# Hybrid encoder layer, one core: first loads in halves on two queues, memory columns turned inside the chunks

## The reference, cut to what matters

```
mkv = mem @ w_mem_kv[l]            # (256 x 2048) @ (2048 x 2048), float32
mk, mv = jnp.split(mkv, 2, axis=-1)
```

## Time and profile before

| | us |
|---|---|
| median of the runs (lowest, highest) | 1850.0 (1849.56, 1850.88) |
| span of the profiled execution | 1848.4 |
| TensorE busy | 1825.4 (99%) |
| VectorE busy | 1311.8 (71%) |
| ScalarE busy | 864.8 (47%) |
| GpSimd busy | 206.5 (11%) |
| mean granted TensorE clock | 0.996 |

### The profile page before, as it was taken

The page is one execution under the profiler, slowest core; times in us unless marked ns, Lnnn a source line. Parts: engine busy times, 40 slices in busy tenths (PEclk is TensorE's granted clock), DMA queues, the critical chain, the costliest instruction groups (busy, mean ns, idle before and its releaser), DMA issues.

```text
span 1848.4 us, 24154 instructions
## 1 busy us (share of the span) xinstructions
PE 1825.4 (99%) x8577; PEld 1512.7 (82%) x8577; DVE 1311.8 (71%) x2076; ACT 864.8 (47%) x1461; POOL 206.5 (11%) x279
## 2 busy tenths in 40 slices
PE   9999999999999999999999999999999999999995
PEld 7888888888888888888888888888888888888884
DVE  5777765887767675566678878878787644576776
ACT  4653333554555554444445545545455333235543
POOL 1111110000111110000000000000001000003223
PEclk9999999999999999999999999999999999999998
DMA  9576677963643433444273360533619445439988
GB/s 327 186 206 179 185 196 219 224 216 78 176 113 97 119 91 109 117 129 129 65 215 105 147 218 25 213 103 126 227 46 319 150 154 178 145 110 233 243 210 192
DMA packets 227415, 301.49 MB, mean 163 GB/s; under 512 B 13633, under 2 KB 140673, under 8 KB 225153
## 3 DMA queue, kind: packets, MB, share of 16 engines
q1 hardware_dynamic: 171824, 188.24, 32.1%
q0 software_dynamic: 55360, 111.61, 22.7%
q10 hardware_dynamic: 144, 0.52, 0.1%
HBM read 247.73 MB, written 50.97 MB: 162 GB/s over the span
## 4 chain that ended last, share of the span: by engine, by line
PE 95%; DMA 2%; ACT 1%; DVE 1%; POOL 1%; issue 0%; DVEq 0%; SPq 0%; POOLq 0%; ACTq 0%
PE acc L667 10%; PE acc L669 10%; PE acc L668 10%; PE scores L862 6%; PE scores L858 6%; PE scores L860 6%; PE acc L862 3%; PE acc L860 3%; PE acc L858 3%; PE transposed L692 3%; PE scores L1102 2%; PE scores L1103 2%; PE scores L1101 2%; PE attended L860 2%; PE attended L862 2%; PE attended L858 2%
## 5 line engine op out<-in xcount | busy, mean ns | idle before, releaser
L1289 ACT ACTIVATE piece_split<-w 128x512 fp32r<-128x512 f32 x448 | 282.5, 632 | 288.8 <-PE scores L862 105.3
L1849 DVE TENSOR_TENSOR piece_split<-w,piece_split 128x512 fp32r<-128x512 f32 x448 | 308.8, 691 | 110.3 <-ACT piece_split L1289 98.5
L1703 DVE TENSOR_TENSOR w_lo<-raw_weights,w_hi 128x1024 fp32r<-128x1024 f32 x181 | 220.3, 1220 | 179.8 <-ACT w_hi L1184 178.8
L667 PE MATMUL acc<-h_hi,w_lo 128*128 128x512 f32 x800 | 319.4, 399 | 0.0
L669 PE MATMUL acc<-h_hi,w_hi 128*128 128x512 f32 x800 | 312.4, 391 | 0.0
L668 PE MATMUL acc<-h_lo,w_hi 128*128 128x512 f32 x800 | 311.6, 389 | 0.0
L1184 ACT ACTIVATE w_hi<-raw_weights 128x1024 fp32r<-128x1024 f32 x181 | 191.2, 1059 | 191.4 <-PE acc L1103 52.2
L669 PEld LDWEIGHTS acc<-h_hi,w_hi 128*128 128x128 f32 x800 | 150.1, 188 | 32.4
L667 PEld LDWEIGHTS acc<-h_hi,w_lo 128*128 128x128 f32 x800 | 150.8, 189 | 29.9 <-issue 1.8
L668 PEld LDWEIGHTS acc<-h_lo,w_hi 128*128 128x128 f32 x800 | 150.6, 188 | 28.4
L858 PE MATMUL scores<-piece_split,h_lo 128*128 128x512 f32 x384 | 149.6, 390 | 0.0
(11 more groups left out here) (447 smaller groups left out, 3677.7 us busy)
## 6 DMA issues: line engine op xcount, KB each, us to landing
w<-in_w_in SPq DMA_DIRECT2D x128, 512.0 KB, 7.4
raw_weights<-in_w_in SPq DMA_DIRECT2D x102, 512.0 KB, 3.8
raw_weights<-in_w_branch SPq DMA_DIRECT2D x48, 512.0 KB, 5.2
raw_weights<-in_w_mem_kv SPq DMA_DIRECT2D x32, 512.0 KB, 6.1
gate<-gate_scratch POOLq DMA_DIRECT2D x12, 1024.0 KB, 6.7
h_sums<-sums_scratch POOLq DMA_DIRECT2D x6, 1024.0 KB, 10.4
gate_scratch<-first_product POOLq DMA_DIRECT2D x12, 512.0 KB, 6.5
out_w_x<-in_w_out POOLq DMA_DIRECT2D x12, 512.0 KB, 7.8
```

What stands on the lines that cost most here:

```text
L667: pe.matmul(bank_out, wl, hi[:, k, :], start=first, stop=False)
L1289: act.activation(p_split[:, n % RING, 0, :], sources[p][:, k, :], ACT.Copy).then_inc(pc_hi, 1)
L1703: dve.tensor_tensor(w_lo[:, slot, :], raw[:, slot, :], w_hi[:, slot, :].bitcast(F32), ALU.subtract).then_inc(lo_ready, 1)
L1849: dve.tensor_tensor(p_split[:, n % RING, 1, :], sources[p][:, k, :], p_split[:, n % RING, 0, :].bitcast(F32), ALU.subtract).then_inc(pc_lo, 1)
```

## The change

Loads. SyncE now issues memory columns 0 to 255 (256 KB), the second half of chunk 0 (256 KB), memory columns 256 to 511 (256 KB), chunks 1 and 2, memory columns 512 to 1023, chunk 3, columns 1024 to 1535, chunk 4, columns 1536 to 2047, chunk 5 and on. The first half of chunk 0 (256 KB) is issued by ScalarE, ahead of its first copy.

TensorE. Six warming matmuls in place of 8, fill 0, five more, chunk 0. Fill 1 stands between the halves of chunk 0, fills 2 and 3 behind the first and the second half of chunk 1, fill 4 behind chunk 2, fills 5 and 6 behind the halves of chunk 3, fill 7 between the halves of chunk 4. Chunk 1 is split and waited for in halves too.

ScalarE and VectorE. The order becomes memory part 0, chunk 0 in halves, memory part 1, chunk 1 in halves, chunk 2, memory part 2, chunk 3, part 3, chunk 4, part 4, chunk 5, part 5, parts 6 and 7, chunk 6 and on.

Semaphores. `ident_made` and the masks' one are one, as are the two of the last half stores; counts are raised to match.

The diff, cut to its core:

```diff
-            load_mem(0)
-            load_k(0)
+            load_mem(0, 1, mem_loaded[0])
+            sp.dma_start(raw[:, 0, 512:CW], w_mem_kv[0][P:2 * P, 0:512]).then_inc(raw_loaded[0], 16)
+            load_mem(1, 2, mem_second_loaded)
             load_k(1)
-            load_mem(1)
             load_k(2)
+            load_mem(2, 4, mem_loaded[1])
             load_k(3)
-            load_mem(2)
-            load_mem(3)
+            load_mem(4, 6, mem_loaded[2])
             for n in range(4, 8 * HC):
                 load_k(n)
+                if n == 4:
+                    load_mem(6, 8, mem_loaded[3])
...
-            for n in range(8):
+            for n in range(6):
                 pe.matmul(ob[:, 0:P], ident[:, :], ident[:, :], start=True, stop=True)
             fill_mem(0)
-            fill_mem(1)
             for n in range(5):
                 pe.matmul(ob[:, 0:P], ident[:, :], ident[:, :], start=True, stop=True)
-            mem_chunk(0)
-            fill_mem(2)
-            fill_mem(3)
-            mem_chunk(1)
-            fill_mem(4)
-            fill_mem(5)
-            mem_chunk(2)
-            fill_mem(6)
-            fill_mem(7)
-            for n in range(3, 8 * HC):
+            mem_chunk(0, {0: lambda: fill_mem(1)})
+            mem_chunk(1, {0: lambda: fill_mem(2), 1: lambda: fill_mem(3)})
+            mem_chunk(2, {1: lambda: fill_mem(4)})
+            mem_chunk(3, {0: lambda: fill_mem(5), 1: lambda: fill_mem(6)})
+            mem_chunk(4, {0: lambda: fill_mem(7)})
+            for n in range(5, 8 * HC):
...
+            act.dma_start(raw[:, 0, 0:512], w_mem_kv[0][0:P, 0:512]).then_inc(first_loaded, 16)
             mem_part(0)
...
+            for n in range(2):
+                act.wait_ge((first_loaded, raw_loaded[1])[n], 16)
+                act.activation(w_hi[:, n, 0:512], raw[:, n, 0:512], ACT.Copy).then_inc(first_hi, 1)
+                act.wait_ge(raw_loaded[n], 16)
+                act.activation(w_hi[:, n, 512:CW], raw[:, n, 512:CW], ACT.Copy).then_inc(hi_ready, 1)
+                if n == 0:
+                    mem_part(1)
+            for n in range(2, 6):
+                split_hi(n - LOOKAHEAD)
+                mem_part(n)
```

## The result

The changed kernel takes 1852.98 us in the median (1852.18 to 1854.57), the kernel before beside it 1850.65 us: ratio 1.0013, 95% interval 1.0008 to 1.0019. It is 2.3 us slower, clear of noise and under 0.2%. The forecast was 1849.8 with a range to 1852.0. It started from a median of 1850.0 for the kernel before; against its own start it allowed for -0.2 us and at most 2.0, and the runs moved by +2.3. The profiled execution spans 1850.5 us against 1848.4.

What follows compares the result with a forecast made beforehand. TensorE's start was taken to bound the kernel: -1.57 us from an earlier chunk 0, +0.44 for fill 1, +0.9 for a wait at chunk 1, in sum -0.2, giving 1849.8 us. The range was 1847.9 to 1852.0.

Steps and rivals of the forecast that it cites:

- Reading of the bound: Whole kernel: a microsecond by which TensorE's first real matmul starts earlier is a microsecond of the result, unless lost in the stream.
- Term 1: First loads, halved and on two queues: memory columns land at 4.6 us, weights at 5.7 (bounds 5.0 to 6.9).
- Rival B: First loads: weights land late, at 6.9, as the second queue doesn't speed them; +0.7 us, 1850.7; chance 0.2.
- Term 2: Start of TensorE: two warming matmuls fewer end the warming 0.9 us earlier, at 4.4, beside the wait for the load.
- rival C: Start of TensorE: slow pace lasts into chunk 0, six matmuls 1.46 us more, fills and copies 0.3 to 0.4; 1851.6; chance 0.1.
- Term 3: Fill 0 to chunk 0's first matmul: 2.9 us, so chunk 0 starts at 7.5; gain so far 1.57 us.
- Terms 4 and 5: Chunks 0 and 1: fill 1 now inside the stream costs 0.44 us, a new wait ahead of chunk 1 costs 0.9.
- term 6: Memory columns 512 to 1023 and 1536 to 2047 load later: nothing, given 4.7 us of slack; otherwise 1.3 us per load.
- Terms 6 and 7: Memory loads moved back in the queue, and semaphores joined: both put at nothing.
- rival D: Chunks 2 to 8: 1 KB pieces or the reordered queue starve the stream; 4 us of loss, 1854; chance 0.03.

Runs made afterwards that it cites:

- e3: Changed kernel with the first half of chunk 0 issued on SyncE's queue, not ScalarE's: 0.7 us faster than before (ratio 0.9985 to 1.0003).
- e13: Changed kernel with SyncE's second and later loads held until ScalarE's first half of chunk 0 landed: 0.2 us slower than before (0.9993 to 1.0012).
- e6: Changed kernel with 17 warming matmuls in place of 6: 3.0 us slower than before (ratio 1.0005 to 1.0023).
- e4: Changed kernel with memory columns 0 to 511 in one load of 2 KB pieces, still two queues: 3.7 us slower than before (1.0010 to 1.0028).
- e7b: Changed kernel with only 32 KB of chunk 0's first half on ScalarE's queue, the rest on SyncE's: 0.7 us faster than before (0.9986 to 1.0004).
- e2: Kernel before with only the new order of work, its loads kept on one queue: 2.0 us slower than before (ratio 1.0002 to 1.0020).
- e9: Kernel before with GpSimd's six small loads held until chunk 0's rows landed: 0.3 us slower than before (ratio 0.9991 to 1.0009).
- e5: Kernel before with chunk 0's rows loaded in two halves on SyncE's queue: 0.4 us faster than before (ratio 0.9990 to 1.0008).
- e1: Kernel before with only the new loads, its order of work kept: 2.7 us slower than before (ratio 1.0003 to 1.0021).

## Why the prediction was wrong, step by step

- **Reading of the bound: right.** TensorE's start is carried through to 1785 us almost unchanged (2.98, then 3.07). What I left out is that the tail, which is bound by loads, gives nearly 1 us back (3.07 late at its first load, the spans 2.1 apart).
- **Term 1, the half-size loads: the step that failed.** I put the columns' landing at 4.6 and gave bounds only to the weights' landing (5.0 to 6.9). It was 7.2 for the columns and 7.1 for the weights. The working added up bytes, as if a load were announced when they and some more had moved; e3 shows that this is nearly so on one queue (3.6, when I had allowed 4.2), and e13 that with two queues it is so only while nothing else is queued (4.7 and 4.9). With the later loads queued it is not. Rival B was nearest, with later loads served among the first ones, but it was priced for the weights alone. Its bound of 6.9, put on the columns, gives 6.9 + 2.9 = 9.8 for chunk 0; the measured start of fill 0 gives 7.3 + 2.9 = 10.2, and 10.54 was measured. That bytes served in between were the cause is itself not shown: up to 4.4 us there were none. The Trainium skill, "DMA: Bandwidth & Descriptors", section "Issuing engines are not separate DMA queues", says that such transfers share the engines and interleave, and that a second issuer saves issue time alone. The runs agree on the saving: ScalarE's load was issued at 0.74, 0.5 us earlier than as SyncE's second in e3. That the columns landed 3.6 us later than on one queue is read from the runs alone.
- **Term 2, two warming matmuls fewer: not free.** The warming ended at 4.46, as summed, and then TensorE idled 2.87 us. The fill and the five matmuls behind it ran at the slow pace, as rival C says: 0.5 us by e6, where it had 0.3 to 0.4 for the fills and their copies; its other 1.46, for the first half of chunk 0, didn't come. In e4 the slow pace reached chunk 0 itself and cost 1.15 more. When the pace rises is partly luck: e3 and e7b give TensorE the same work without a break from 1.53 on, and the ten short matmuls behind fill 0 took 2.13 us in e3 and 1.28 in e7b. The Trainium skill, "TensorE: Matmul & The Clock Gate", Part 1, which has the low level as the default that activity releases, agrees with these rows.
- **Term 3, fill to matmul: right.** 2.9 summed; 2.71 in e6, 3.16 in e3, 3.21 in the changed kernel, the longer two at the slow pace.
- **Terms 4 and 5: right in size.** 0.44 for fill 1, and 0.88 for the wait ahead of chunk 1 (0.9 summed), seen in e2, e3 and the changed kernel alike. These two left an early landing with little to gain: e7b starts chunk 0 1.76 us earlier than before and is 0.26 us ahead at the column turn. e3 starts it 1.66 us earlier and is 0.2 us later there, because it loses 0.36 us more in a term that I had put at nothing (term 6).
- **Terms 6 and 7: right for the changed kernel,** in which no matmul waits for a load after chunk 1. With an early start it isn't so: in e3 fill 2 waits for memory columns 512 to 1023, whose load moved back (rival D's mechanism), and starts 1.77 us after chunk 1 where e7b's starts after 1.47; from chunk 0 to the column turn e3 takes 21.14 us, e7b 20.78.

The sum with measured terms: fill 0 2.22 later; less 0.75, since from fill 0 to chunk 0 it took 3.96 before (the weights were late) and 3.21 after; 0.44 and 0.88 for fill 1 and the wait; 0.2 unaccounted (in e2 as well). Together 3.0 us at the column turn, of which 2.3 are left at the end of the runs.

## What to carry to other kernels

Before splitting the first loads over two queues, ask what stands queued behind them: here the columns landed at 7.2 us with later loads queued, at 4.9 with none, and at 3.6 on one queue with all of them. A small share on the second queue did no harm (32 KB: 3.7, 128 KB: 3.9). And when work is moved from an idle stretch into a full stream, count the chain that it starts: of the 1.76 us that the earliest chunk 0 gave (e7b), 1.3 went to the moved fill and the new wait, 0.2 is unaccounted, and 0.26 was left at the column turn.

## What the runs showed of the hardware that was not expected

- With 256 KB on a second queue at the start, the first 256 KB of SyncE's queue landed at 7.2 us; with one queue at 3.6; with two, and nothing behind the first loads, at 4.9. One 512 KB load on a second queue, issued at 8.04 us, did no such harm (378 GB/s from 9 to 13 us).
- The delay is there before a byte of the later loads has moved: by 4.4 us 175 and 102 packets of the two first loads had been started in the changed kernel, 257 and 142 in e13, in which nothing else was queued.
- The first loads are slow by themselves: 146 GB/s on the mean over the first 5 us in the kernel before and 142 in e9, without the six small loads beside them; from 7 to 8 us it was 400 and 404, from 8 to 13 us 374 and 395.
- A half load behind a full one was announced at the same time as the whole (7.5 us in e5, 7.54 before); one comparison.
- TensorE's matmuls started 0.43 us apart up to 13.4 us in e4, with an idle stretch of 3.4 us that ended at 7.86, while the profile shows a granted clock of 1.00 for the stretch. In e1, with idle stretches of 2.20 and 0.79 us ahead of its first two fills, the profile does show it: 0.66 on the mean from 8 to 13 us.
